# The beginning of a two-block transformer kernel: x first on the queues, mem turned in the second head group

## The reference

```python
cos, sin = _rope_tables(positions)                       # 256 angles per frequency
for layer in range(2):
    proj = einsum('bsd,de->bse', x, w_in[layer])         # z, xbc, dt, q, k, v, gates ...
    y_ssd = _ssd_branch(z, xbc, dt_raw, ...)             # 5-tap conv, silu, scan over 32 heads in 4 groups
    q, k = _apply_rope(dq, cos, sin), _apply_rope(dk, cos, sin)
    o = _diff_attention(q, k, v, lam)
    mem_kv = einsum('bmd,de->bme', mem, w_mem_kv[layer]) # mem: 256 x 1024
    oc = _memory_cross_attention(cq, mem_kv)
    x = _layernorm(alpha * x + out, ln_g[layer], ln_b[layer])
```

## Time and profile before

| | |
|---|---|
| median of 3 runs | 2441.19 us (2440.38 to 2445.71) |
| the profiled execution | 2443.01 us, its span 2441.1 us |
| TensorE busy | 2391.5 us, 98% of the span |
| VectorE, ScalarE, GpSimd busy | 1713.4, 1339.5, 90.2 us |
| mean granted TensorE clock | 0.994 of full speed |
| data moved | 380.19 MB, 156 GB/s |

### The profile page before, as it was taken

One profiled execution on the slowest core, in us unless ns is written; L12 is line 12 of the kernel. 1 busy time (PEld: TensorE's weight loads), 2 busy tenths in 40 slices (PEclk: granted clock), 3 DMA queues, 4 the chain that ended last, 5 costly groups with the idle time before them and its releaser, 6 DMA issues.

```text
span 2441.1 us, 48177 instructions
## 1 busy us (share of the span) xinstructions
PE 2391.5 (98%) x18842; PEld 2289.4 (94%) x18842; DVE 1713.4 (70%) x2517; ACT 1339.5 (55%) x2355; POOL 90.2 (4%) x101
## 2 busy tenths in 40 slices
PE   9999999999999999999999999999999999999998
PEld 8898999999899999999999997899999999789998
DVE  7788777777888867786766575676566657667665
ACT  6788655644678855563444445554444444555443
POOL 0000000000100000000100010010001001001000
PEclk9999999999999999999999999999999999999999
DMA  7454555455354455545455553345545544434553
GB/s 216 131 159 126 165 164 161 154 170 189 108 153 139 137 156 160 169 155 181 145 181 174 169 160 106 121 144 178 170 147 179 178 163 152 123 124 142 189 181 113
DMA packets 401046, 380.19 MB, mean 156 GB/s; under 512 B 28223, under 2 KB 397037, under 8 KB 400765
## 3 DMA queue, kind: packets, MB, share of 16 engines
q1 hardware_dynamic: 397821, 373.87, 48.0%
q10 hardware_dynamic: 3072, 4.20, 0.7%
HBM read 372.77 MB, written 1.05 MB: 153 GB/s over the span
## 4 chain that ended last, share of the span: by engine, by line
PE 79%; DVE 12%; ACT 3%; DVEq 3%; issue 1%; SPq 1%; DMA 1%; ACTq 0%
PE ps L583 22%; PE ps L585 21%; PE ps L584 21%; DVE scratch L1806 3%; DVE w_lo L1583 3%; DVEq L1805 2%; PE ps L805 2%; PE ps L836 1%; PE ps L837 1%; PE ps L838 1%; ACT scratch L1082 1%; ACT w_hi L1082 1%; PE ps L854 1%; PE ps L612 1%; PE ps L614 1%
## 5 line engine op out<-in xcount | busy, mean ns | idle before, releaser
L1583 DVE TENSOR_TENSOR w_lo<-raw,w_hi 128x1024 fp32r<-128x1024 f32 x664 | 812.0, 1229 | 423.2 <-ACT w_hi L1082 421.8
L583 PE MATMUL ps<-x_hi,w_hi 128*128 128x256 f32 (+1 forms) x3664 | 1056.4, 288 | 4.3 <-DVE w_lo L1583 1.6
L584 PE MATMUL ps<-x_lo,w_hi 128*128 128x256 f32 (+1 forms) x3664 | 1042.6, 285 | 0.0
L585 PE MATMUL ps<-x_hi,w_lo 128*128 128x256 f32 (+1 forms) x3664 | 1039.8, 284 | 0.0
L1082 ACT ACTIVATE w_hi<-raw 128x1024 fp32r<-128x1024 f32 x664 | 697.7, 1056 | 447.5 <-PE ps L585 370.6
L583 PEld LDWEIGHTS ps<-x_hi,w_hi 128*128 128x128 f32 x3664 | 690.8, 189 | 30.8 <-issue 25.3
L584 PEld LDWEIGHTS ps<-x_lo,w_hi 128*128 128x128 f32 x3664 | 692.2, 189 | 2.0
L585 PEld LDWEIGHTS ps<-x_hi,w_lo 128*128 128x128 f32 x3664 | 693.6, 189 | 0.0
L583 PE MATMUL ps<-big_r,w_hi 128*128 128x272 f32 (+1 forms) x832 | 238.9, 287 | 0.0
L585 PE MATMUL ps<-big_r,w_lo 128*128 128x272 f32 (+1 forms) x832 | 238.2, 286 | 0.0
L1082 ACT ACTIVATE scratch<-ps 128x256 f32<-128x256 f32 (+9 forms) x328 | 122.3, 384 | 154.9 <-PE ps L838 63.8
(11 more groups left out here) (302 smaller groups left out, 3063.1 us busy)
## 6 DMA issues: line engine op xcount, KB each, us to landing
raw<-in_w_in SPq DMA_DIRECT2D x184, 512.0 KB, 4.7
raw<-in_ffn_w_up SPq DMA_DIRECT2D x176, 512.0 KB, 4.3
raw<-in_ffn_w_down SPq DMA_DIRECT2D x64, 512.0 KB, 4.2
raw<-in_mix_w_in SPq DMA_DIRECT2D x64, 512.0 KB, 4.6
scratch<-in_w_in SPq DMA_DIRECT2D x40, 512.0 KB, 4.8
raw<-in_w_mem_kv SPq DMA_DIRECT2D x32, 512.0 KB, 4.8
raw<-in_w_br_ssd SPq DMA_DIRECT2D x32, 512.0 KB, 3.8
raw<-in_ffn_w_down SPq DMA_DIRECT2D x32, 384.0 KB, 3.3
```

The lines of the kernel that those rows point to most:

```text
L583: mm(out, wh, xh, start=first, stop=False)
L584: mm(out, wh, xl, start=False, stop=False)
L585: return mm(out, wl, xh, start=False, stop=last)
L1583: tt(w_lo[:, p % PARTS, :, :], raw_at(slot_of(Q, p))[:, :, (p % 2) * P:(p % 2 + 1) * P], wh_f[:, p % PARTS, :, :], ALU.subtract).then_inc( ...
```

## The change

- SyncE: x comes right behind the identity, then positions and frequencies, the first unit of weights. The second unit waits until x has landed. Behind it come dt's weights of layer 0 and the four broadcasts, then the third unit, which no longer waits for mem; behind that the constant tables up to K_MEAN and the late rows. The tables from K_MEAN on, mem, and dt's weights of layer 1 come behind unit 5.
- ScalarE issues the seven row loads.
- mem's tokens lie in `gates`, not in `scratch`. TensorE turns mem in four parts before tiles 0, 2, 4 and 6 of group 1, all in bank 5, each part waiting for VectorE's subtraction of the part before. ScalarE copies before tiles 0, 2, 4 and behind tile 5, VectorE subtracts likewise.
- The angles are computed by GpSimd, in 15 operations, in `big`. ScalarE makes sinT and cosT behind the split of tile 1 in group 0.
- TensorE's dt tiles come behind tile 4 instead of tile 2, VectorE's `dt_exponent` at tile 3, ScalarE's exponential at tile 4.
- Products of zeros: 8 before x, 8 behind it, none elsewhere (before: 4, 4 and 8).

```diff
-            for src, dst, s in ((a["mem"][0], mem_tok, mem_in), (a["x"][0], x_tok, x_in)):
+            tokens_in(a["x"][0], x_tok, x_in)
+            load(pos_in, pos_i, spread(a["positions"][0]))
+            const_cols(K_INV, 5, pos_in)
...
                     cols(Q, 0, l, "w_in", X0 + g * 512)
                     if l == g == 0:
-                        early_params()
+                        sp.wait_ge(x_in[1], 16)
                     cols(Q, 1, l, "w_in", X0 + 256 + g * 512)
                     if l == g == 0:
+                        step_params()
+                    if g == 0 and l:
+                        sp.wait_ge(S["merged_ready"], l * 4)
+                    halves(Q, 2, l, "w_in", B0 + g * P, C0 + g * P)
+                    if l == g == 0:
                         late_params()
-                    if g == 0:
-                        if l == 0:
-                            sp.wait_ge(S["mem_ready"], 4)
...
                         cols(Q, 5 + j, l, "w_in", GL0 + 256 * j + g * 768)
+                        if l == g == j == 0:
+                            const_cols(K_MEAN, K_INV - K_MEAN, late_tabs_in)
+                            const_cols(K_SUB, P, late_tabs_in)
+                            tokens_in(a["mem"][0], mem_tok, mem_in)
+                            step_weights(1)
...
+            pts, ptt = pool.tensor_scalar, pool.tensor_tensor
+            pool.wait_ge(pos_in, 32)
+            pool.tensor_copy(red[:, 2, :], pos_i)
...
+            for c in (C1, C2, C3):
+                pool.drain()
+                pts(red[:, 1, :], red[:, 3, :], -c, None, ALU.mult)
+                pool.drain()
+                ptt(an, red[:, 1, :], an, ALU.add)
...
-            idle_products(ps[7], WARM_MEM)
+            idle_products(ps[7], WARM_X)
             pe.wait_ge(ident_in, 16)
-            turn_tokens(mem_tok, mem_banks, mem_in, "mem_turned")
-            idle_products(ps[7], WARM_X)
             turn_tokens(x_tok, x_banks, x_in, "x_turned")
-            pe.wait_ge(S["mem_ready"], 1)
             idle_products(ps[5], WARM_W)
-            pe.wait_ge(S["mem_ready"], 4)
+
+            def turn_mem(b):
+                pe.wait_ge(mem_in[b // 2], 16)
+                if b:
+                    pe.wait_ge(S["mem_ready"], b)
+                for f in range(2 * b, 2 * b + 2):
+                    for t in range(2):
+                        m = pe.transpose(ps[5][:, (f % 2) * SEQ + t * P:(f % 2) * SEQ + (t + 1) * P], mem_tok[:, t, f * P:(f + 1) * P], ident)
+                m.then_inc(S["mem_turned"], 1)
...
+                        if l == 0 and g == 1 and k in (0, 2, 4, 6):
+                            turn_mem(k // 2)
                         proj(Q, T, k, k, x1, own=ps[5] if g == 0 and k == 3 else None)
+                        if l == g == 0 and k == 4:
+                            dt_tiles()
...
+            def mem_copy(b):
                 act.wait_ge(S["mem_turned"], b + 1)
-                copy(mem_hi[:, 2 * b:2 * b + 2, :], pair(mem_banks[b])).then_inc(S["mem_hi_ready"], 1)
+                copy(mem_hi[:, 2 * b:2 * b + 2, :], pair(ps[5])).then_inc(S["mem_hi_ready"], 1)
...
                     for j in range(6):
+                        if l == 0 and g == 1 and j in (0, 2, 4):
+                            mem_copy(j // 2)
                         done(T, j)
...
                         split(Q, j + 4)
+                        if l == g == 0 and j == 1:
+                            rope_tables()
...
                     for j in range(6):
+                        if l == 0 and g == 1 and j in (0, 2, 4):
+                            mem_rest(j // 2)
                         conv(j)
                         split(Q, j + 4)
                         if j:
                             conv_silu(j - 1)
-                        if g == 0 and j == 1:
+                        if g == 0 and j == (1 if l else 3):
                             dt_exponent()
+                    if l == 0 and g == 1:
+                        mem_rest(3)
                     conv_silu(5)
```

More of the change, by code:

```diff
@@ L84 @@
 WARM = 30
-WARM_MEM, WARM_X, WARM_W = 4, 4, 8
+WARM_X, WARM_W = 8, 8
 SETUP_H = 0
@@ L384, in _, with tokens_in @@
             const_cols(K_ID, P, ident_in)
-            load(pos_in, pos_i, spread(a["positions"][0]))
-            const_cols(K_INV, 5, pos_in)
-            for src, dst, s in ((a["mem"][0], mem_tok, mem_in), (a["x"][0], x_tok, x_in)):
+            def tokens_in(src, dst, s):
                 for h in range(2):
@@ L390, in _ @@
                     sp.dma_start(dst[:, :, c], src.rearrange("(t p) d -> p t d", p=P)[:, :, c]).then_inc(s[h], 16)
[L392 to L398, removed]
@@ L400, in late_params @@
-            def late_params():
[L401 to L404, removed]
-                    if l == 0:
[L406 to L409, removed]
+            tokens_in(a["x"][0], x_tok, x_in)
@@ new lines, in _, with step_weights, step_params @@
+            load(pos_in, pos_i, spread(a["positions"][0]))
+            const_cols(K_INV, 5, pos_in)
+            def step_weights(l):
+                load(w_dt_in[l], w_dt[:, l, :, :], a["w_in"][l].rearrange("(k p) c -> p k c", p=P)[:, :, DT0:DT0 + 64])
+            def step_params():
+                step_weights(0)
+                for dst, src in ((neg_a, a["a_log"]), (dt_bias, a["dt_bias"])):
+                    load(params_in, dst.rearrange("p l n -> p (l n)"), spread(src.rearrange("l d h -> (l d h)")))
+                load(params_in, skip_all.rearrange("p l n -> p (l n)"), spread(a["d_skip"].rearrange("l h -> (l h)")))
+                load(params_in, lam_in.rearrange("p l n -> p (l n)"), spread(a["diff_lam"].rearrange("l a b -> (l a b)")))
@@ L1136, in pair, with load, rope_tables @@
                 return bank[:, :].rearrange("p (f s) -> p f s", f=2)
-            for b in range(4):
-                act.wait_ge(S["mem_turned"], b + 1)
-                copy(mem_hi[:, 2 * b:2 * b + 2, :], pair(mem_banks[b])).then_inc(S["mem_hi_ready"], 1)
-            act.wait_ge(S["angles_ready"], 1)
-            fn(sinT[:, :], red[:, 0, :], ACT.Sin, scale=const[:, K_SIGN:K_SIGN + 1])
-            fn(cosT[:, :], red[:, 1, :], ACT.Sin).then_inc(S["rope_ready"], 1)
+            def load(s, dst, src):
+                act.dma_start(dst, src).then_inc(s, 16)
+            load(rows_in, rows_a[0:PA_ROWS, :, :], a["conv_w"].rearrange("l k (t p) -> (k t) l p", p=P))
+            for at, src in ((PB_CONVB, a["conv_b"]), (PB_NORM, a["ssd_norm_w"]), (PB_LNG, a["ln_g"]),
+                            (PB_LNB, a["ln_b"]), (PB_DNW, a["diff_norm_w"])):
+                n = src.shape[1] // P
+                load(rows_in, rows_b[at:at + n, :, :], src.rearrange("l (t p) -> t l p", p=P))
+            load(rows_in, rows_b[PB_GATE:PB_GATE + 24, :, :], a["gate_b"].rearrange("l b (t p) -> (b t) l p", p=P))
+            def mem_copy(b):
+                act.wait_ge(S["mem_turned"], b + 1)
+                copy(mem_hi[:, 2 * b:2 * b + 2, :], pair(ps[5])).then_inc(S["mem_hi_ready"], 1)
+            def rope_tables():
+                act.wait_ge(S["angles_ready"], 1)
+                fn(sinT[:, :], red[:, 0, :], ACT.Sin, scale=const[:, K_SIGN:K_SIGN + 1])
+                fn(cosT[:, :], red[:, 1, :], ACT.Sin).then_inc(S["rope_ready"], 1)
             def x_first(b):
@@ L1192, in _ @@
             dt_weights(0)
+            act.wait_ge(S["idle_ready"], 1)
             for l in range(DEPTH):
@@ L1226, in _ @@
                                 late_copies()
-                        if g == 0 and j == 2:
+                        if g == 0 and j == (2 if l else 4):
                             act.wait_ge(S["dt_pre"], l + 1)
@@ L1238, in z_tile @@
                         split(Q, 6 + j + 4)
+                    if l == 0 and g == 1:
+                        mem_copy(3)
                     z_tile(0)
@@ L1589, in _, with mem_rest @@
             v.sem_inc(lo_ready, LO_CREDIT)
[L1590 to L1608, removed]
             def pair(bank):
                 return bank[:, :].rearrange("p (f s) -> p f s", f=2)
-            for b in range(4):
+            def mem_rest(b):
                 v.wait_ge(S["mem_hi_ready"], b + 1)
                 t = slice(2 * b, 2 * b + 2)
-                tt(mem_lo[:, t, :], pair(mem_banks[b]), mem_hi[:, t, :].bitcast(F32), ALU.subtract).then_inc(S["mem_ready"], 1)
+                tt(mem_lo[:, t, :], pair(ps[5]), mem_hi[:, t, :].bitcast(F32), ALU.subtract).then_inc(S["mem_ready"], 1)
             def x_rest(b):
```

49 lines of the change are left out of this document (32 added, 17 removed).

## The result

The changed kernel took 2448.84 us (2444.91 to 2451.35, 14 runs) against 2442.90 for the kernel before (2440.38 to 2445.71, 14 runs): ratio 1.0024, 95% interval 1.0016 to 1.0031. It is 5.9 us slower. I had forecast 2.2 us faster, and the time lies outside my range. The profiled execution has a span of 2446.7 us (before 2441.1). In what follows each ratio is to runs of the kernel before taken beside that experiment; one run of e3 (4669.11 us), one of e4 (2873.52) and one of the kernel before beside e1 to e4 (4660.30) lie far above all others and count in the medians but not in the ratios.

What follows compares the result with a forecast made beforehand. The prediction took TensorE, busy 98% of the span, to bound the kernel. A gain of 5.5 us up to `cumulate` and a loss of 3.3 us for mem in group 1 gave -2.2 us: 2439.0 us, range 2435.5 to 2443.0.

Steps and rivals of the forecast that it cites:

- TensorE's chain: First projection to `cumulate`, group 0: same tiles reordered, 38.7 us from 13.8 to 52.5, so 5.5 us gained.
- the step on the sine tables: ScalarE, tile 1 of group 0: one table load and two activations add 2.2 us before the tap of tile 2.
- VectorE's chain: Group 0 up to a_tok: conv(2) starts at 30.0, a_tok comes at 51.4, 6.4 us earlier than 57.8.
- The clock behind the dt tiles: Half clock right behind the narrow dt matmuls: still costs 1.7 us, left in and only moved.
- Start of the projections: First projection at 13.8 (12.7 to 15.3) instead of 18.06, a gain of 4.3 us (2.8 to 5.4).
- my term: Loads at the start: positions and seven row loads delay the first weights by 0.9 us.
- The third unit: Third unit of weights: issued between 11 and 16, there at 18 to 22.8, no wait on TensorE's chain.
- mem in group 1: Turning mem between group 1's tiles: waits of 1.35 and 1.45 us, 3.3 us lost (bounds 1.9 and 6.9).
- GpSimd's angles: Rival, chance 0.08: 15 angle operations from 6.6 end between 17.7 and 28.7, late end holding ScalarE 4.8 us: 2442.7.
- A slow clock at the first projection: Rival, chance 0.20: idle TensorE before the first projection drops the clock to 1.2 GHz, costing 1.7 us: 2440.7.
- The serial hand-over: Rival, chance 0.09: mem's four parts in group 1 go serially through one bank, 6.9 us instead of 3.3: 2442.6.
- More than I gave: Rival, chance 0.15: weights at 10.0, start at 12.7, no slow stretch behind the dt tiles, 7.7 - 3.3 = -4.4: 2436.8.

Runs made afterwards that it cites:

- e3: The changed kernel with 12 products of zeros put in TensorE's wait before tile 4: 2452.22 us, ratio 1.0039 to the kernel before.
- e4: The changed kernel with ScalarE's sine tables made behind z tile 2 of the first group: 2443.76 us, ratio 1.0006 to the kernel before.
- e1: The changed kernel with the dt tiles and their counterparts on VectorE and ScalarE back behind tile 2: 2442.77 us, ratio 1.0000 to the kernel before.
- e2: The changed kernel with tile 4 of the first group waiting only for the copy of tile 0: 2442.26 us, ratio 1.0000 to the kernel before.
- e8: The changed kernel with the seven row loads issued by SyncE behind the first unit of weights: 2448.07 us, one run.
- e10: e9 with one dt tile behind tile 3, one behind tile 4, and 15 products of zeros behind x instead of 8: 2436.34 us, ratio 0.9975.
- e9: The changed kernel with e2, e4, e5 and e8 together, mem copied twice by ScalarE and subtracted between head pairs: 2440.31 us, ratio 0.9985.
- e5: The changed kernel with mem's parts turned alternately in banks 5 and 2, each waiting for the subtraction two parts earlier: 2448.15 us, one run.

## Why the prediction was wrong, by its steps

- *TensorE's chain, "the same tiles in another order and so the same 38.7 us".* This step failed. I checked that the weights of tile 4 would be split in time and did not check its other wait, for its bank. The move took away the cover of the copy of tile 2, which I had myself delayed by 2.2 us in the step on the sine tables: I put that delay on VectorE's chain only. By my own times the wait was there to be seen: conv(2) at 30.0 stands 0.7 us behind the end of that copy (33.4 and 34.09 in the changed kernel), so the copy ended at 29.3, and tile 4 was due at 25.7, an estimate of 3.6 us. Measured: 48.3 us instead of 38.7, of which 5.6 are idle and 4.0 more than before are lost to the clock. e1 and e2, which give tile 4 its cover back or take the wait away, both bring back the time of the kernel before.
- *The clock behind the dt tiles, "I leave it in, only moved".* Wrong in size: one stretch of 3.4 us at half clock before, two of 6.8 us after. Nearly all of tile 4 ran in the first.
- *Start of the projections.* Direction right, size half: 2.25 us instead of 4.3. x's second half landed at 8.9, not 7.3, and the first weights were used at 13.40, not 11.1. 15.81 lies beyond even the late end of my bounds. The row loads are not the whole of it: with the rows behind the first unit (e8 to e10) the weights were used at 11.70 to 12.18, where I had 10.0 for rows that cost nothing. So about 2 us of the delay lie in the landings of x and the weights themselves, and the share of the rows is 0.2 to 2.3 us (my term: 0.9). The rule of the Trainium skill that I weighed there ("DMA: Bandwidth & Descriptors", Issuing engines are not separate DMA queues), that loads of all issuers share the same DMA engines, agrees with e8 (x's second half in 4.7 us against 7.2), less so with e9 and e10 (5.6 and 5.2).
- *The third unit.* I had it at 18 to 22.8; ScalarE had it at 25.12 and waited 2.43. SyncE issued it at 15.02, as I had said; it took 10 us, not 6.8.
- *VectorE's chain.* I had a_tok at 51.4; it came at 62.6. conv(2) began at 34.09 instead of 30.0, and `dt_exponent` then waited 4.2 us for the late dt tiles. It still ended 1.5 us ahead of TensorE's tile 9 (64.14), so there was no wait before `cumulate`, as forecast.
- *mem in group 1.* Right: 3.3 us forecast, 2.76 measured; waits of 1.35 and 1.45 forecast, 1.22 and 1.37 measured, none before part 1.
- *The rivals.* GpSimd's angles ended at 27.7, just before ScalarE asked at 28.1: 17.2 us for 15 operations, near the middle of my two ends, but begun at 10.48 instead of 6.6. The two longest operations (1.64 us, at 16.46 and 19.46) stood beside VectorE's weight splits; its x splits, which I had named too, were over at 11.7. A slow clock at the first projection came in seven of the ten experiments, not in the changed kernel's own profile. The serial hand-over did not come. None of the rivals was the mechanism that decided, a bank's wait whose cover was moved. (In *More than I gave* the signs are turned: -7.7 + 3.3 = -4.4.)

## What to carry to other kernels

When work is moved off a place, ask what it was hiding there: list every semaphore that the next instruction waits for, not only the one that looks nearest, and find when each is raised. A count that is shared by tiles in different banks makes a tile wait for a copy that has nothing to do with it. Here the idle TensorE was paid twice, once in time and once in the clock of the full tile behind it, and so was the block of narrow matmuls; with the block in halves the second price was gone (1.7 us, e10).

## What the runs showed that I had not expected

- 48 matmuls of 64 columns in a row had a granted clock of 0.50 (1.2 GHz) from within the block or right behind it, in both layers and in every profile, although TensorE was busy throughout; the one exception is layer 0 of e10, with 24 and 24 and a full tile between.
- At the start of the projections the clock stayed full behind idles of TensorE of 2.08, 2.26 and 2.33 us (e2, e4, the changed kernel) and fell to 0.50 with those of 2.37 to 2.97 us (e1, e3 and e5 to e9).
- A table load of ScalarE took 1.28 us, and two activations for sine between others cost two of them: 3.55 us for 0.9 of work (e4).
- A 512 KB load issued ahead of small loads on a second queue took 5.6 to 7.2 us, without them 4.7 to 5.6 (e8 to e10): the ranges meet, so the size of the delay is open.
- GpSimd's single-source operation on 128x256 took 0.41 to 1.64 us, the two longest beside VectorE's splits.
